# A hybrid decoder step on one core: expert rows scattered once into a sorted table, and two combinations of a pair moved around the SwiGLU transposes

## The chip, the cores and the metric

The kernel runs on one core of a Trainium2 chip. Its time is the device time of one launch in microseconds (us); lower is better. The core has TensorE (PE in the profile, PEld for its weight loads), VectorE (DVE), ScalarE (ACT), GpSimd (POOL), SyncE (SP, which here only issues transfers) and 16 DMA engines, which all queues share. All arithmetic is in float32.

## The reference, cut to what matters

One layer runs over 288 tokens: 256 of a prompt and 8 sequences of 4. After two attention-like branches and an output projection, the second half of the layer is a mixture of experts. It is the part that the change touches:

```python
def hier_moe(h, w_grp, b_grp, w_exp, b_exp, w_gate_e, w_up_e, w_down_e):
    ...                                  # top group of 4, top 2 of its 4 experts
    combine = jnp.sum(jax.nn.one_hot(expert_id, N_EXPERTS) * top_w[..., None], axis=1)
    a = jnp.einsum('td,edf->tef', t, w_gate_e)
    u = jnp.einsum('td,edf->tef', t, w_up_e)
    hid = jax.nn.silu(a) * u * combine[..., None]
    return jnp.einsum('tef,efd->td', hid, w_down_e)
```

There are 16 experts, D = 2048 and 512 hidden columns. The weights of one expert are 12.6 MB (three matrices of 2048 x 512), and the layer ends in a gated residual and an RMSNorm.

## The kernel before, in words

The kernel is written engine by engine, with semaphores; nothing reorders it. Each engine runs its own block from top to bottom, so the order of the code is the order of its queue.

Large weights come through a ring of six slots of 2 MB, loaded by SP. Over the program these are the six uses that matter here: the weights w_up_a and w_up_b ("UP", eight loads, lines 424 to 450), w_out (eight loads) and, from line 464 on, six loads per expert: gate and up of the first half of D, gate and up of the second half, and two halves of the down matrix. A load waits until PE has released the slot (`ring_free`), so the ring runs about one expert ahead of PE.

The experts are computed in *turns*. A turn takes up to 64 rows (W = 64) of one expert; an expert with more rows gets more turns, and the table `wtab` says which expert a turn has (up to 26 turns, NWIN = 26; this input needs 16). Two turns make a *pair*, and the PE loop of line 1180 runs over pairs. One turn on PE is:

1. gate and up products, 16 steps over D, two matmuls each, against the rows `hs` (lines 1186 to 1194);
2. `turn_rows`: 16 transposes of `hg`, the gathered rows of the next turn, into PSUM, from where ACT copies them to `hs`;
3. four transposes of `hid`, the SwiGLU result that DVE has made meanwhile (hid_ready), which DVE copies to `hidT`;
4. the down products, whose result ACT and DVE copy into `y_two`: one turn's 64 rows in each half of the partitions.

Rows go back to their tokens with `combine(pair, n)`, n = 0 to 7: two products of `y_two` with a matrix `spots` that has the router's weight where a row belongs to a token. DVE then adds the result to the residual `xT` (`add_pair`, line 2085), and only after that may PE start the next `combine` (`combined_read`), since all use PSUM banks 6 and 7. All eight combinations of the pair before stand between the gate and up steps of a pair's first turn.

Where the rows come from: after the router, PE turns the normalised tokens into rows, ACT copies them to `hTok`, and POOL stores them in token order in DRAM (`h_rows`, three transfers, line 625). DVE works out for each of the two choices of a token its expert's turn (`at_turn`) and its place in it (`at_slot`), PE sums them up to a list per turn (`lists_summed`), and for each turn POOL gathers 64 rows from `h_rows` by an indirect transfer (`gather`, line 627), once PE has turned the rows of the turn before. Gathered rows land in partitions 0 to 63 of `hg`.

Of the kernel before, what the change touches and what calls it, by code (L numbers as in the profile page):

```python
# [11 lines left out]
ALU = mybir.AluOpType  # L12
# [51 lines left out]
        "kv_tok_ready gla_scratch_free f_ready s_new_copied ob_ready work_free ms2_ready logits_copied member_ready pos_ready "  # L64
        "table_ready list_ready").split(),
# [7 lines left out]
def build(nc, io, out):  # L73
    with ExitStack() as ctx:
# [52 lines left out]
        h_rows = nc.dram_tensor("h_rows", [T, D], F32).ap()  # L127
# [121 lines left out]
        token_i = rstd[0:W, 0:NWIN].bitcast(I32)  # L249
        take = rstd[0:W, 64:65].bitcast(I32)  # L250
# [77 lines left out]
        def _(sp):  # L328
# [134 lines left out]
            def expert(e, turn):  # L463
# [12 lines left out]
            last_turn = sp.value_load(wtab[0:1, 1:2], min_val=NE - 1, max_val=NWIN - 3)  # L476
            with sp.Fori(0, last_turn) as w:
                e = sp.value_load(wtab[0:1, ds(w + 3, 1)], min_val=0, max_val=NE - 1)
                expert(e, w + 1)
# [11 lines left out]
        def _(pool):  # L491
# [122 lines left out]
            pool.dma_start(xflat, x_kept).then_inc(sem("x_back"), 16)  # L614
            pool.iota(iota_pos[:, :], pattern=[[1, T]], base=0, channel_multiplier=0, allow_small_or_imprecise_dtypes=True)
# [16 lines left out]
            pool.wait_ge(sem("h_stored"), 16 * NT)  # L632
            pool.wait_ge(*step("list_ready"))
            gather(0)
            pool.wait_ge(sem("hs_turned"), 1)
            gather(1)
# [3 lines left out]
            last_turn = pool.value_load(wtab[0:1, 1:2], min_val=NE - 1, max_val=NWIN - 3)  # L640
# [9 lines left out]
        def _(pe):  # L650
# [529 lines left out]
            with pe.Fori(0, pairs) as pair:  # L1180
                for half_turn in range(2):
# [22 lines left out]
                    last.then_inc(sem("hid_turned"), 1)  # L1204
                    pe.wait_ge(sem("hidT_ready"), it + 1)
# [251 lines left out]
        def _(v):  # L1457
# [582 lines left out]
            pick(at_slot, within)  # L2040
            tt(in_slot, slot_no.unsqueeze(1).to_broadcast([TT, 6, 2 * W]), at_slot.unsqueeze(2).to_broadcast([TT, 6, 2 * W]), ALU.is_equal)
            pick(at_turn, turn)
# [12 lines left out]
            v.drain()  # L2055
            for n in range(2):
                tt(listing[:, :, :, n], in_turn, entry[:, :, n:n + 1].to_broadcast([TT, 6, NWIN]), ALU.mult)
# [17 lines left out]
            copy(token_i, sums[0:W, :, 0])  # L2075
            copy(listed, sums)
            v.drain()
            v.sem_inc(reach("list_ready"), 1)

            nc.vector.memset(spots, 0.0)  # L2080
            v.wait_ge(sem("h_stored"), 16 * NT)
# [21 lines left out]
            with v.Fori(0, pairs) as pair:  # L2103
                for half_turn in range(2):
# [3 lines left out]
                    if half_turn == 0:  # L2108
                        for n in range(8):
                            add_pair(pair, n)  # L2110
# [7 lines left out]
                    copy(now[rows], listed[rows, ds(it, 1), :].rearrange("p w n -> p (w n)"))  # L2118
                    v.drain()
                    tsc(spots[rows], iota_pos[rows], now[rows, 0:1], now[rows, 1:2], ALU.is_equal, ALU.mult)  # L2120
                    v.wait_ge(sem("hid_turned"), it + 1)
                    copy(hidT, ps[:, 3, 0:4 * W].rearrange("p (f t) -> p f t", f=4)).then_inc(sem("hidT_ready"), 1)
# [42 lines left out]
```

## Time and profile before

| what | value |
| --- | --- |
| median of 3 runs | 1935.51 us (1934.56 to 1939.46) |
| span of the profiled execution | 1934.0 us (the page gives no other time of it) |
| PE busy | 1767.3 us, 91% |
| DVE, ACT, POOL busy | 28%, 11%, 8% |
| DMA moved | 531.09 MB, mean 275 GB/s |
| chain that ended last | PE 65%, issue 12%, DMA 10%, DVE 5% |
| UP and w_out stages | about 1055 to 1328 us of the span |
| router | about 1337 to 1374 us |
| loop over pairs | 1377.55 to 1904 us |
| end | to 1934.0 us |

PE is busy in nearly all of the program, but "busy" holds matmuls at either clock and with waits inside. A stage is read by what ends its waits, and by whether the DMA engines are full in it.

### The profile page before, as it was taken

The numbers are of one execution on the slowest core, as the hardware profiler recorded it, in microseconds if no ns is written. First come the engines' busy times: TensorE is split into PE (matmuls) and PEld (weight loads), VectorE is DVE, ScalarE is ACT, GpSimd is POOL, SyncE is SP. The second block draws the span as 40 slices with busy tenths as digits, with TensorE's granted clock in tenths as the row PEclk, the third lists the DMA queues.
The fourth block names the chain that finished last, engine by engine and source line by source line (L and its number), as shares of the span: only waits on it lengthen the run. The fifth ranks groups of instructions, "written<-read, shape, count | busy, mean of one in ns | idle before, by whom it ended". The sixth has DMA issues, their size and how long they took to land.

```text
span 1934.0 us, 27785 instructions
## 1 busy us (share of the span) xinstructions
PE 1767.3 (91%) x11144; PEld 1114.0 (58%) x11144; DVE 534.1 (28%) x1152; ACT 210.8 (11%) x405; POOL 156.1 (8%) x274
## 2 busy tenths in 40 slices
PE   7799999999998999978889999997699998998998
PEld 4366666666666877756667777775333333333335
DVE  3100000000047744455553111003323222231233
ACT  2010000000001201102222100002110001000002
POOL 1011111111110001410000000000100000000000
PEclk9899999999999999988899999998799899999999
DMA  9997887677516335538999874242499999999992
GB/s 371 402 380 273 317 297 285 246 262 289 198 49 201 100 111 168 207 119 298 385 392 368 325 271 134 88 174 94 146 368 406 397 397 384 410 404 383 401 391 96
DMA packets 154570, 531.09 MB, mean 275 GB/s; under 512 B 17701, under 2 KB 61899, under 8 KB 131803
## 3 DMA queue, kind: packets, MB, share of 16 engines
q1 hardware_dynamic: 128834, 432.24, 58.9%
q0 software_dynamic: 17088, 97.15, 14.1%
q10 hardware_dynamic: 8578, 0.73, 0.4%
q8 instruction: 49, 0.80, 0.2%
q14 instruction: 21, 0.17, 0.0%
HBM read 510.94 MB, written 19.15 MB: 274 GB/s over the span
## 4 chain that ended last, share of the span: by engine, by line
PE 65%; issue 12%; DMA 10%; DVE 5%; SPq 4%; DVEq 1%; POOL 1%; ACT 1%; POOLq 1%; ACTq 0%; PEldq 0%
PE ps L652 62%; DMA ring<-in_w_up_e_dram 4%; DMA ring<-in_w_ada_dram 2%; PE ps L662 2%; SPq L399 2%; DMA xT<-in_w_ada_dram 2%; SPq L393 2%; DMA xT<-in_w_in_dram 2%; POOL work L537 1%; DVE z L1468 1%; DVE z L1459 1%; DVEq L2115 1%; DVE ring L1465 1%; POOLq L536 0%; DVE ring L1837 0%
## 5 line engine op out<-in xcount | busy, mean ns | idle before, releaser
L652 PE MATMUL ps<-hT,ring 128*128 128x288 f32 x2304 | 585.3, 410 | 5.3 <-PE ps L652 3.6
L652 PEld LDWEIGHTS ps<-hT,ring 128*128 128x128 f32 x2304 | 430.0, 190 | 169.7 <-issue 59.1
L652 PE MATMUL ps<-ring,work 128*64 128x512 f32 (+1 forms) x1280 | 273.4, 617 | 25.3 <-DMA ring<-in_w_ada_dram 12.2
L652 PE MATMUL ps<-z,ring 128*128 128x288 f32 (+1 forms) x1040 | 255.5, 407 | 4.5 <-PE ps L652 2.7
L1468 DVE COPY z<-ps 128x256 f32<-128x256 f32 (+7 forms) x98 | 64.3, 660 | 677.1 <-PE ps L652 656.9
L652 PE MATMUL ps<-ring,z 32*32 32x256 f32 (+3 forms) x3744 | 213.9, 396 | 21.2 <-DVE z L1468 11.2
L652 PEld LDWEIGHTS ps<-z,ring 128*128 128x128 f32 x1040 | 196.4, 190 | 62.8 <-issue 7.5
L652 PEld LDWEIGHTS ps<-ring,work 128*64 128x64 f32 (+1 forms) x1280 | 77.8, 134 | 181.4 <-issue 165.7
L652 PEld LDWEIGHTS ps<-ring,z 32*32 32x32 f32 (+3 forms) x3744 | 108.5, 114 | 115.2 <-issue 108.3
L1263 ACT ACTIVATE z<-ps 128x512 f32<-128x512 f32 (+4 forms) x108 | 60.1, 602 | 860.3 <-PE ps L652 850.4
L1465 DVE SCALAR_TENSOR_TENSOR xT<-ps,modT,xT 128x256 f32<-128x256 f32 x160 | 70.8, 480 | 254.3 <-PE ps L652 254.2
L662 PE MATMUL ps<-ident,z 64*128 64x64 f32 (+4 forms) x644 | 91.3, 286 | 40.9 <-DVE z L1459 29.6
L662 PEld LDWEIGHTS ps<-ident,z 64*128 64x128 f32 (+4 forms) x644 | 75.7, 177 | 64.4 <-issue 48.8
L652 PE MATMUL ps<-z 128*128 128x288 f32 (+3 forms) x408 | 109.2, 393 | 2.5 <-DVEq L2126 1.5
L652 PE MATMUL ps<-hT,xT 128*128 128x288 f32 (+1 forms) x352 | 86.6, 409 | 24.7 <-DMA xT<-in_w_in_dram 24.7
L652 PEld LDWEIGHTS ps<-z 128*128 128x128 f32 (+1 forms) x408 | 64.4, 188 | 71.6 <-DVEq L2096 47.0
L652 PEld LDWEIGHTS ps<-hT,xT 128*128 128x128 f32 (+1 forms) x352 | 65.9, 203 | 43.9 <-DMA xT<-in_w_in_dram 26.4
L1263 ACT ACTIVATE work<-ps 128x512 f32<-128x512 f32 (+1 forms) x75 | 36.7, 513 | 384.7 <-PE ps L652 336.4
L1837 DVE STREAM_TRANSPOSE ring<-ring 128x2048 f32<-128x2048 f32 x32 | 72.3, 2293 | 8.0 <-issue 3.7
L628 POOL COPY rstd<-rstd 64x1 int32 (+1 forms) x17 | 3.2, 189 | 471.3 <-PE ps L662 461.8
L1459 DVE TENSOR_TENSOR hT<-hT,ps 128x288 f32<-128x288 f32 x32 | 14.5, 454 | 89.5 <-PE ps L652 88.7
L1863 DVE CUSTOM_DVE_ANT_0 xT<-ps,z 128x1024 f32<-128x1024 f32 x16 | 20.5, 1283 | 67.2 <-PE ps L652 65.9
(209 smaller groups left out, 877.4 us busy)
## 6 DMA issues: line engine op xcount, KB each, us to landing
ring<-in_w_in_dram SPq DMA_DIRECT2D x36, 2048.0 KB, 14.3
ring<-in_w_gate_e_dram SPq DMA_DIRECT2D x32, 2048.0 KB, 12.7
ring<-in_w_up_e_dram SPq DMA_DIRECT2D x32, 2048.0 KB, 18.4
ring<-in_w_down_e_dram SPq DMA_DIRECT2D x32, 2048.0 KB, 15.0
ring<-in_w_ada_dram SPq DMA_DIRECT2D x16, 2048.0 KB, 20.5
z<-in_w_ada_dram POOLq DMA_DIRECT2D x32, 1024.0 KB, 7.9
xT<-in_w_ada_dram POOLq DMA_DIRECT2D x32, 1024.0 KB, 6.7
ring<-in_cache_v_dram SPq DMA_DIRECT2D x64, 512.0 KB, 5.8
```

The lines of the kernel that those rows point to most:

```text
L393: pg = sp.value_load(ptab[0:1, ds(b * NPG + (s % 2 * 4 + n), 1)], min_val=0, max_val=io["cache_k"].shape[1] - 1)
L399: sp.dma_start(slot(s)[:, n * 1024:(n + 1) * 1024], io[name][0, ds(pg, 1)].rearrange("a p h d -> (a p) (h d)")).then_inc(sem(f"kv_full{s}" ...
L537: pool.dma_start(lf_in[:, ds(i * 2 + k // NPG, 1), k % NPG, :].rearrange("p a h -> p (a h)"), io["cache_logf"][0, ds(pg, 1)].rearrange("a ...
L652: return nc.tensor.matmul(o, lhsT, rhs, start=start, stop=stop, skip_group_check=free)
L662: return nc.tensor.transpose(o, i, ident[0:n, 0:n])
L1263: return nc.scalar.activation(o, i, func, **kw)
L1459: return nc.vector.tensor_tensor(o, a, b, op)
L1465: return nc.vector.scalar_tensor_tensor(out=o, in0=a, scalar=s, in1=b, op0=op0, op1=op1)
L1468: return nc.vector.tensor_copy(o, a)
L1837: nc.vector.transpose(kT[:, g, 4 * half:4 * half + 4], slot(half).rearrange("p (n g e) -> p n g e", n=4, g=2)[:, :, g]).then_inc(sem("keys ...
L1863: nc.vector.tensor_tensor_reduce(pS[:, g, 0:PAST].rearrange("p (a m) -> p a m", a=4), ps[:, 0:4, g * 256:(g + 1) * 256], r_turn[:, g, :].r ...
L2115: v.drain()
```

## The change

There are two parts.

First, the rows. A DRAM table `h_sorted` of 26 x 64 rows takes the place of `h_rows`. POOL fills it with zeros once (a memset of 128 x 1024, and 13 transfers of 1 MB each, right after `xT` is fetched back). When DVE has the place of each choice (`places` = turn x 64 + slot), POOL scatters the rows of `hTok` into it, six indirect transfers of 96 rows, one for each third of the tokens and each choice. SP then fetches 64 consecutive rows for a turn with a plain transfer: the first two ahead of the loop, and in the loop between the gate and up loads and the down loads of an expert. POOL's loop is gone, as are DVE's cast of the list and the signal `list_ready`. DVE picks `at_turn` before it makes `in_slot`.

Second, the order. Of the eight combinations of a pair, numbers 6 and 7 leave the gate and up steps. Number 6 now stands between `turn_rows` and the transposes of `hid`, number 7 behind these transposes. DVE's `add_pair` 6 and 7 are moved to match, and the making of `spots` goes behind them.

```diff
-            for c in range(NT):
-                pool.wait_ge(sem("htok_copied"), 4 * c + 4)
-                pool.dma_start(h_rows[c * TT:(c + 1) * TT, :], hTok[:, c, :]).then_inc(sem("h_stored"), 16)
-            def gather(w):
-
-                pool.tensor_copy(take, token_i[:, ds(w, 1)])
-                pool.drain()
-                pool.indirect_dma_start(hg, None, h_rows, bass.IndirectOffsetOnAxis(ap=take, axis=0)).then_inc(sem("hg_full"), 16)
...
+            pool.memset(cleared, 0.0)
+            pool.drain()
+            for n in range(NWIN * W // P):
+                pool.dma_start(h_sorted[n * P:(n + 1) * P, :].rearrange("p (a n) -> p a n", a=2),
+                               cleared.unsqueeze(1).to_broadcast([P, 2, 1024])).then_inc(sem("rows_cleared"), 16)
...
+            pool.wait_ge(*step("places_ready"))
+            pool.wait_ge(sem("htok_copied"), 4 * NT)
+            pool.wait_ge(sem("rows_cleared"), 16 * (NWIN * W // P))
+            for i in range(2 * NT):
+                pool.indirect_dma_start(h_sorted, bass.IndirectOffsetOnAxis(ap=places[:, i:i + 1], axis=0),
+                                        hTok[:, i // 2, :], None).then_inc(sem("rows_sorted"), 16)
...
-            with pool.Fori(0, last_turn) as it:
-                pool.wait_ge(sem("hs_turned"), it + 2)
-                gather(it + 2)
...
+            def sorted_rows(turn):
+
+                sp.dma_start(hg, h_sorted[ds(turn * W, W), :]).then_inc(sem("hg_full"), 16)
...
+                    if n == 4 and rows_of is not None:
+                        sp.wait_ge(sem("hs_turned"), rows_of)
+                        sorted_rows(rows_of)
...
             expert(0, 0)
+            sp.wait_ge(sem("rows_sorted"), 16 * 2 * NT)
+            sorted_rows(0)
+            sp.wait_ge(sem("hs_turned"), 1)
+            sorted_rows(1)
...
-                            if k % 2 and half_turn == 0:
-                                combine(pair, 4 * half + k // 2)
+                            n = 4 * half + k // 2
+                            if k % 2 and half_turn == 0 and n < 6:
+                                combine(pair, n)
...
                     turn_rows()
+                    if half_turn == 0:
+                        combine(pair, 6)
                     pe.wait_ge(sem("hid_ready"), it + 1)
...
                     last.then_inc(sem("hid_turned"), 1)
+                    if half_turn == 0:
+                        combine(pair, 7)
...
             pick(at_slot, within)
+            pick(at_turn, turn)
+            stt(places, at_turn, float(W), at_slot, ALU.mult, ALU.add)
+            v.drain()
+            v.sem_inc(reach("places_ready"), 1)
...
-            v.wait_ge(sem("h_stored"), 16 * NT)
+            v.wait_ge(sem("rows_sorted"), 16 * 2 * NT)
             nc.vector.memset(y_two, 0.0)
```

On PE the place is the end of a pair's first turn. The rows "128x64" are transposes (16 of the next rows, four of `hid`), "128x288" a combination, "ring,work" gate and up, "ring,z" down. Before:

```order
L652 MATMUL ps<-z 128x288 [waits combined_read]
L652 MATMUL ps<-z 128x288
L652 MATMUL ps<-ring,work 64x512 x4
L1170 REGISTER_ALU
L652 MATMUL ps<-z 128x288 [waits combined_read]
L652 MATMUL ps<-z 128x288
L1197 REGISTER_ALU
L662 MATMUL ps<-ident,z 128x64 [waits hg_full]
L662 MATMUL ps<-ident,z 128x64 x15
L662 MATMUL ps<-ident,z 128x64 [waits hid_ready]
L662 MATMUL ps<-ident,z 128x64 x3
L1210 REGISTER_ALU [waits y_copied_too,y_copied,hidT_ready]
```

and now:

```order
L656 MATMUL ps<-ring,work 64x512 x8
L1202 REGISTER_ALU
L666 MATMUL ps<-ident,z 128x64 [waits hg_full]
L666 MATMUL ps<-ident,z 128x64 x15
L1174 REGISTER_ALU
L656 MATMUL ps<-z 128x288 [waits combined_read]
L656 MATMUL ps<-z 128x288
L666 MATMUL ps<-ident,z 128x64 [waits hid_ready]
L666 MATMUL ps<-ident,z 128x64 x3
L1174 REGISTER_ALU
L656 MATMUL ps<-z 128x288 [waits combined_read]
L656 MATMUL ps<-z 128x288
```

Two combinations have left the gate and up steps; one now stands ahead of the wait for `hid`, one behind the transposes of `hid`.

On POOL the place is the router, from the fetching back of `xT` to the loop. "DMA h_sorted<-work" is the clearing, "DMA h_sorted<-z,rstd" the scatter. Before:

```order
L614 DMA xT<-x_kept 128x4608 [waits dve_step]
L615 IOTA z 128x288
L616 AFFINE_SELECT z<-ones 96x96
L618 IOTA work 96x6
L620 IOTA z 96x128
L625 DMA h_rows<-z 96x2048 [waits htok_copied] x3
L628 COPY rstd<-rstd 64x1 [waits dve_step,h_stored]
L630 DMA z<-h_rows,rstd 64x2048
L628 COPY rstd<-rstd 64x1 [waits hs_turned]
L630 DMA z<-h_rows,rstd 64x2048
```

and now:

```order
L625 DMA xT<-x_kept 128x4608 [waits dve_step]
L626 MEMSET work 128x1024
L629 DMA h_sorted<-work 256x1x1024 x13
L631 IOTA z 128x288
L632 AFFINE_SELECT z<-ones 96x96
L634 IOTA work 96x6
L636 IOTA z 96x128
L643 DMA h_sorted<-z,rstd 1664x2048 [waits rows_cleared,htok_copied,dve_step]
L643 DMA h_sorted<-z,rstd 1664x2048 x5
```

Thirteen transfers are added behind `xT`'s, and six scatters stand where three stores and the first gathers stood.

On SP the place is the loop over experts. Now it reads:

```order
L479 DMA ring<-in_w_gate_e_dram 128x4096
L479 DMA ring<-in_w_up_e_dram 128x4096 [waits ring_free1]
L472 REGISTER_ALU
L465 ISA [waits hs_turned]
L465 DMA z<-h_sorted 64x2048
L474 REGISTER_ALU
L479 DMA ring<-in_w_down_e_dram 128x4096 [waits ring_free2]
L479 DMA ring<-in_w_down_e_dram 128x4096 [waits ring_free3]
```

The wait for `hs_turned` and the fetch stand in SP's queue ahead of the two down loads; before, the down loads followed the up load directly.

## Rows read from the trace of the kernel before

**Rows 1.** Page, part 1: span and instructions of the profiled execution.
```profile
span 1934.0 us, 27785 instructions
```

**Rows 2.** Windows: length; PE, PEld, DVE, ACT, POOL busy; PE clock, DMA share, GB/s.
```profile
1442.80:1840.50 397.70, 363.85 (x1586) 145.63 (x1583) 111.30 (x277) 33.36 (x49) 15.45 (x24) 0.95 1.01 396
...
1840.50:1904.00 63.50, 59.76 (x264) 23.84 (x264) 17.17 (x46) 4.37 (x7) 1.45 (x2) 0.95 0.80 320
```

**Rows 3.** Waits from 1375 to 1900: engine line <- waited for: total, times, longest.
```profile
PE ps L662 <- DVE z L1459: 18.3, 16, 1.8
...
PE ps L652 <- DMA ring<-in_w_up_e_dram: 11.7, 4, 4.1
PE ps L652 <- DVE z L1468: 11.2, 16, 0.8
```

**Rows 4.** DMA queues from 1375 to 1900: packets, MB, share of 16 engines.
```profile
q1 hardware_dynamic: 12960, 188.75, 89.6%
```

**Rows 5.** DMA queues from 1448 to 1466, weights alone.
```profile
q1 hardware_dynamic: 523, 7.72, 100.7%
```

**Rows 6.** Windows of 2 us: first turn, and the end of the weights' stream.
```profile
1392.00:1394.00 2.00, 2.00 (x10) 0.49 (x8) 1.24 (x4) 0.00 (x0) 0.00 (x0) 1.00 0.85 254
1402.00:1404.00 2.00, 2.00 (x11) 0.80 (x8) 0.76 (x4) 0.50 (x1) 0.00 (x0) 1.00 0.35 147
1404.00:1406.00 2.00, 2.00 (x17) 1.61 (x15) 1.30 (x5) 0.09 (x1) 0.00 (x0) 1.00 0.80 246
...
1890.00:1892.00 2.00, 2.00 (x12) 0.61 (x10) 0.00 (x0) 0.00 (x0) 0.00 (x0) 1.00 0.41 172
```

**Rows 7.** Windows of 0.5 us while x_sample's 32 rows pass SP's queue.
```profile
8.50:9.00 0.50, 0.00 (x0) 0.00 (x0) 0.07 (x1) 0.39 (x1) 0.00 (x0) 1.00 1.00 411
9.00:9.50 0.50, 0.00 (x0) 0.00 (x0) 0.50 (x1) 0.00 (x0) 0.00 (x0) 1.00 1.38 303
9.50:10.00 0.50, 0.00 (x0) 0.00 (x0) 0.50 (x1) 0.00 (x0) 0.00 (x0) 1.00 0.81 148
10.00:10.50 0.50, 0.00 (x0) 0.00 (x0) 0.50 (x1) 0.00 (x0) 0.00 (x0) 1.00 0.90 197
10.50:11.00 0.50, 0.00 (x0) 0.00 (x0) 0.50 (x1) 0.00 (x0) 0.00 (x0) 1.00 1.00 279
```

**Rows 8.** Windows of 2 us: the first gather, alone on the DMA engines.
```profile
1370.00:1372.00 2.00, 0.00 (x0) 0.00 (x0) 0.00 (x0) 0.00 (x0) 0.00 (x0) 0.50 0.91 213
1372.00:1374.00 2.00, 0.00 (x0) 0.00 (x0) 0.00 (x0) 0.00 (x0) 0.00 (x0) 0.50 0.22 49
```

**Rows 9.** Timeline of router and loop start: start us, us, engine, line, [idle before].
```profile
1360.29 0.25 DVE L1961 TENSOR_REDUCE work<-work 96x6 f32<-96x96 f32 x1
...
1368.74 0.98 POOL L630 DMA_INDIRECT z<-h_rows,rstd  x1 [1.15 <-issue]
...
1374.15 2.03 PE L662 MATMUL ps<-ident,z 64*128 64x64 f32 x16 [7.25 <-DMA z<-h_rows,rstd]
```

**Rows 10.** DMA queues from 1351 to 1364: three stores of 96 rows each.
```profile
q0 software_dynamic: 336, 2.36, 57.4%
```

**Rows 11.** Timeline of a first turn's end.
```profile
1467.05 2.00 PE L662 MATMUL ps<-ident,z 64*128 64x64 f32 x16
...
1470.86 0.66 PE L662 MATMUL ps<-ident,z 64*128 64x64 f32 x4 [1.81 <-DVE z L1459]
...
1472.12 8.57 PE L652 MATMUL ps<-ring,z 128*64 128x512 f32 x32 [0.59 <-DVE z L1468]
```

**Rows 12.** DMA queues from 1090 to 1096: xT coming back beside UP loads.
```profile
q0 software_dynamic: 111, 1.88, 74.1%
q1 hardware_dynamic: 130, 0.55, 22.2%
```

**Rows 13.** DMA queues from 1080 to 1100.
```profile
q1 hardware_dynamic: 2006, 4.67, 64.7%
```

**Rows 14.** Timeline of PE in UP: 64 matmuls for a load, the fifth.
```profile
1132.96 15.76 PE L652 MATMUL ps<-z,ring 128*128 128x288 f32 x64 [0.30 <-PE ps L652]
```

More of the change, by code:

```diff
@@ L63 @@
         "gla_sample_ready os_turned_copied ms_a_ready rs_a_ready rs_a_inverted "
-        "kv_tok_ready gla_scratch_free f_ready s_new_copied ob_ready work_free ms2_ready logits_copied member_ready pos_ready "
-        "table_ready list_ready").split(),
+        "kv_tok_ready gla_scratch_free f_ready s_new_copied ob_ready work_free ms2_ready logits_copied member_ready places_ready pos_ready "
+        "table_ready").split(),
 }
@@ L125, in build @@
         eps_col = vcol[:, 150:151]
-        h_rows = nc.dram_tensor("h_rows", [T, D], F32).ap()
+        h_sorted = nc.dram_tensor("h_sorted", [NWIN * W, D], F32).ap()
         x_kept = nc.dram_tensor("x_kept", [P, KT * T], F32).ap()
@@ L248, in build @@
         now = ms[:, 2 * NWIN:2 * NWIN + 2]
-        token_i = rstd[0:W, 0:NWIN].bitcast(I32)
-        take = rstd[0:W, 64:65].bitcast(I32)
+        places = rstd[0:TT, 0:2 * NT].bitcast(I32)
+        cleared = work2[:, 0:1024]
         spots = z[:, 3 * D:3 * D + T]
@@ L460, in _, with expert @@
                              src.rearrange("(k p) n -> p k n", p=P)).then_inc(sem(f"ring_full{(WOUT + n) % SLOTS}"), 16)
-            def expert(e, turn):
+            def sorted_rows(turn):
+                sp.dma_start(hg, h_sorted[ds(turn * W, W), :]).then_inc(sem("hg_full"), 16)
+            def expert(e, turn, rows_of=None):
                 for n in range(6):
                     s = (MOE + n) % SLOTS
+                    if n == 4 and rows_of is not None:
+                        sp.wait_ge(sem("hs_turned"), rows_of)
+                        sorted_rows(rows_of)
                     sp.wait_ge(sem(f"ring_free{s}"), turn + freed(MOE + n))
@@ L478, in _ @@
                 e = sp.value_load(wtab[0:1, ds(w + 3, 1)], min_val=0, max_val=NE - 1)
-                expert(e, w + 1)
+                expert(e, w + 1, w + 2)
             for c in range(NT):
@@ L622, in _ @@
             pool.sem_inc(sem("route_consts_ready"), 1)
-            for c in range(NT):
-                pool.wait_ge(sem("htok_copied"), 4 * c + 4)
-                pool.dma_start(h_rows[c * TT:(c + 1) * TT, :], hTok[:, c, :]).then_inc(sem("h_stored"), 16)
-            def gather(w):
-                pool.tensor_copy(take, token_i[:, ds(w, 1)])
-                pool.drain()
-                pool.indirect_dma_start(hg, None, h_rows, bass.IndirectOffsetOnAxis(ap=take, axis=0)).then_inc(sem("hg_full"), 16)
[L632 to L636, printed above, removed]
+            pool.wait_ge(*step("places_ready"))
[4 more added lines that the diff above has]
+                                        hTok[:, i // 2, :], None).then_inc(sem("rows_sorted"), 16)
             pool.wait_ge(sem("htok_turned"), 4 * NT)
@@ L639, in _ @@
                                vcol[:, V_GF:V_GF + KT].unsqueeze(2).to_broadcast([P, KT, P]), ALU.mult).then_inc(sem("gf_spread"), 1)
-            last_turn = pool.value_load(wtab[0:1, 1:2], min_val=NE - 1, max_val=NWIN - 3)
-            with pool.Fori(0, last_turn) as it:
-                pool.wait_ge(sem("hs_turned"), it + 2)
-                gather(it + 2)
             pool.wait_ge(sem("gla_prompt_stored"), 16)
@@ L2040, in _ @@
             pick(at_slot, within)
+            pick(at_turn, turn)
+            stt(places, at_turn, float(W), at_slot, ALU.mult, ALU.add)
+            v.drain()
+            v.sem_inc(reach("places_ready"), 1)
             tt(in_slot, slot_no.unsqueeze(1).to_broadcast([TT, 6, 2 * W]), at_slot.unsqueeze(2).to_broadcast([TT, 6, 2 * W]), ALU.is_equal)
-            pick(at_turn, turn)
             tt(in_turn, iota_pos[0:TT, 0:NWIN].unsqueeze(1).to_broadcast([TT, 6, NWIN]), at_turn.unsqueeze(2).to_broadcast([TT, 6, NWIN]), ALU.is_equal)
@@ L2055, in _ @@
             v.drain()
+            v.wait_ge(sem("rows_cleared"), 16 * (NWIN * W // P))
             for n in range(2):
@@ L2074, in _ @@
             v.wait_ge(*step("lists_summed"))
-            copy(token_i, sums[0:W, :, 0])
             copy(listed, sums)
-            v.drain()
-            v.sem_inc(reach("list_ready"), 1)
             nc.vector.memset(spots, 0.0)
-            v.wait_ge(sem("h_stored"), 16 * NT)
+            v.wait_ge(sem("rows_sorted"), 16 * 2 * NT)
             nc.vector.memset(y_two, 0.0)
@@ L2108, in _ @@
                     if half_turn == 0:
-                        for n in range(8):
+                        for n in range(6):
                             add_pair(pair, n)
@@ L2118, in _ @@
                     copy(now[rows], listed[rows, ds(it, 1), :].rearrange("p w n -> p (w n)"))
+                    if half_turn == 0:
+                        add_pair(pair, 6)
+                    v.wait_ge(sem("hid_turned"), it + 1)
+                    copy(hidT, ps[:, 3, 0:4 * W].rearrange("p (f t) -> p f t", f=4)).then_inc(sem("hidT_ready"), 1)
+                    if half_turn == 0:
+                        add_pair(pair, 7)
                     v.drain()
                     tsc(spots[rows], iota_pos[rows], now[rows, 0:1], now[rows, 1:2], ALU.is_equal, ALU.mult)
-                    v.wait_ge(sem("hid_turned"), it + 1)
-                    copy(hidT, ps[:, 3, 0:4 * W].rearrange("p (f t) -> p f t", f=4)).then_inc(sem("hidT_ready"), 1)
                     v.wait_ge(*used(MOE + 4, it))
```

## Prediction

> **What bounds the kernel now.** I read the page first: a span of 1934.0 us [rows 1]. The median of the runs is 1.5 us above it; sums are made against the span, and the difference is applied to 1935.5. Then the loop, by windows. In pairs 1 to 6 the DMA engines are full: share 1.01 at 396 GB/s [rows 2]. The waits name DMA only four times, 11.7 us in all, beside 29.5 us for DVE's work on `hid` (18.3 and 11.2) [rows 3]. That looks like a PE-bound loop, but the two are tied: PE frees a slot, the load queues, and six pairs take 397.7 us, 66.3 each, while pair 7, whose loads have mostly run out (share 0.80), takes 63.5 [rows 2]. So the middle goes at the pace of the transfers, and PE has about 3 us per pair to spare.
>
> What a pair's transfers take: 15 experts load 188.75 MB [rows 4], 25.2 MB per pair. Weights alone pass at 7.72 MB in 18 us, 429 GB/s [rows 5], so 58.7 us of 66.3. The other 7.6 us are two gathers, 3.8 us each, for 0.52 MB that at 429 GB/s would take 1.2. The whole stream agrees: it runs from 1392.0 to about 1890.8, idle for some 1.7 us in the first turn [rows 6]; 497 less 188.75 / 0.429 = 440 leaves 57 for 15 gathers.
>
> **The rows: what it costs ahead of the loop.** Before, PE starts on the first rows at 1374.15 [rows 9]. Now:
> - `places`: DVE's reduction for `at_slot` ends at 1360.54 [rows 9]. A multiply and a reduction for `at_turn`, 0.25 each as that one, and a small operation, with their drains: 1361.5.
> - POOL takes some 0.8 us to the first scatter. The gather issued at 1368.74 had its bytes moving at about 1370.2 [rows 8, 9], so the scatter's move from about 1363.8.
> - The scatter moves 2 x 288 rows of 8 KB, 4.72 MB. No row shows an indirect store. The stores of the same 96-partition rows moved 2.36 MB in 57.4% of 13 us, 7.5 us, 316 GB/s [rows 10]: 14.9 us, to 1378.7. The bounds: 429 GB/s gives 11 us [rows 5]. The other end is the gather's pace: its 64 rows took some 3.1 us from 1370.2 until about 0.9 us before PE had them at 1374.15, so 576 rows need 28 us [rows 8, 9]. I take 14.9, the nearest row by partitions and direction. POOL's issue, 0.98 us for 64 rows [rows 9], is 9 us for 576 and lies beside it.
> - Receipt about 1 us, then SP's fetch: issue and first byte 1.0, 2.3 for the bytes (0.91 + 0.22 of 2 us windows, the gather alone [rows 8]), receipt 1: 1384.2.
>
> That is 10.0 us late (6 to 23), and nothing hides it: the engines and queues are idle there. DVE's memset of `y_two` now waits for the scatter too, but ends near 1382, ahead of the first combination. The queue's pauses earlier in the router stay.
>
> **The clearing.** 13.6 MB of writes follow `xT` on POOL's queue from about 1096, in pieces of 4 KB, beside UP loads in pieces of 2 KB. In [rows 12] the engines served 111 pieces of 18 KB and 130 of 2 KB, about one for one: at 1.2 small per large (2.4 KB against 4), UP loads keep 37% of 400 GB/s, 145. They have to deliver, in order, 7.5 MB by 1133.0, when PE turns to the fifth load [rows 14], and 5.4 MB by 16.1 us earlier, 1116.9. By 1100 they had moved 4.67 MB [rows 13], so at 1096 about 3.2; 2.2 MB at 145 GB/s is 15 us, 1111, and the next at 1125. Then clearing ends near 1150 with loads still 8 us early. I take 0; with UP loads at 75 GB/s, somewhat under what they had in [rows 12], the second would be 5 us late, so 6 us is the upper end. The Trainium skill (DMA: Bandwidth & Descriptors, Queues, rings and completion order) says that an engine goes round its queues by packets of several descriptors. By it the share could come out more even, and the cost would still be 0; no row here separates the two.
>
> **The fetch in the loop.** The gather on POOL's queue goes; 64 rows of 8 KB come on SP's queue, behind the gate and up loads. The bytes and the 64 partitions are the same. Its new cost is bounded below by the gather alone, 2.3 us [rows 8], and above by the 3.8 of now. The nearest row is x_sample: 32 rows of 8 KB to 32 partitions, in line on SP's queue among large loads. In the 2 us from 9.0 the mean is 232 GB/s against 411 [rows 7]: 0.87 us lost, 0.64 for its own bytes, 1.5 us. Twice is 3.0, with ragged edges counted twice. I take 2.8: 1.0 us less per turn, for 14 turns (the last is not waited for), 14.0. Nor is it late: it lands 2.8 us behind the second gate and up loads, and PE works 7 us on these. SP's new wait for `hs_turned` holds up only the down loads; their slots come free later still, since PE turns the rows before the down products.
>
> The Trainium skill (SBUF — State Buffer, Door 1: The DMA port swizzle) says that partitions 0 to 63 reach only half of the ports, about 218 GB/s, whatever queue issues. The trace agrees: 213 GB/s in the gather alone [rows 8]. By it the fetch takes 2.4 us, and moving it to SP's queue does not make it faster by itself; what can be saved is the loss of mixing.
>
> **The combinations.** Before, PE ends the row transposes at 1469.05, waits 1.81 us for `hid`, 0.59 for `hidT`, and then has 8.57 us of down products [rows 11], where turns at full clock throughout need about 7.1. The granted clock fell to its lower level (1.2 GHz) behind these waits; that is some 4 us. Combination 6 now fills the first wait, 7 the second, but 7 must wait until DVE has read 6, about 1 us. I count 3 us saved on PE per pair. The work of the combinations is the same, only moved. But PE already has slack: a pair of transfers will be 58.7 + 5.6 = 64.3 us, PE's own pair 63.5 - 3 = 60.5. So these 3 us go into waiting for DMA. What remains: in the first turn the second half's slots come free 2.6 us earlier, which removes the 1.7 us of idle queue [rows 6]. Bounds: 0 and 24 (8 x 3).
>
> **Sum.** +10.0 + 0 - 14.0 - 1.7 = -5.7 us; the span to 1928.3, the median to 1929.8.
>
> **The rivals.**
> - *Fetching costs what the gather cost* (3.8 us): the loss would be in the partitions, not in the mixing. Then the loop gains only 1.7 and perhaps 1.5 at its end. +7: 1942.5. For it: bytes and partitions are the same. Against: the gather alone and x_sample are both cheaper per row.
> - *The scatter goes at the gather's pace* and takes 28 us, not 15: +13, net +7.6, 1943. This is the slower side as one mechanism: its place is the wait of SP ahead of the first fetch, and it decides from a scatter of about 20.6 us on. For it: the only indirect transfer seen ran slower than the plain stores. Against: a gather writes to 64 partitions, the scatter reads from 96.
> - *The loop is PE's after all*, as the waits read [rows 3]: 8 x 3 = 24 saved, +10: 1921.5. Against: share 1.01 over six pairs [rows 2].
> - *Clearing starves UP*: +6, 1936.
>
> **Chances.** Forecast 0.47 (its own range 1922 to 1937), fetching as dear 0.14, slow scatter 0.15, PE's loop 0.14, starved UP 0.06, something else 0.04. A measurement tells 0.3% (5.8 us) from no change, so faster means below 1929.7, slower above 1941.3. The forecast lies on that border: about half of it and nearly all of PE's loop are faster, 0.41; slower are most of the two dear cases, 0.24; the rest 0.35. Eight in ten: 1919 to 1945.
>
> **What would show it.** The first `turn_rows` at about 1384 (later: the scatter). DMA share still 1.0 in the loop, and pairs of about 64.3 us; 66 would be the first rival, 61 the third. No more 2 us windows at 250 GB/s of 5 or 6 us length, but shorter dips. PE's waits for `hid` gone in first turns, waits for DMA longer instead. UP without a DMA wait. It would be wrong if the loop's length did not change, or the head cost over 20 us.

## The result and the profile after

The changed kernel takes 1975.0 us (median of 4 runs, 1969.5 to 1977.6) where the kernel before takes 1935.7: a ratio of 1.0195, interval 1.0174 to 1.0215. That is 45 us over the forecast of 1929.8, and outside its range.

The profiled executions are 42.1 us apart, the medians 39.4. The page's first line [rows 1], PE's first row transposes behind the router, and its last down products in the loop:

```profile
span 1976.1 us, 27750 instructions
...
1388.29 2.03 PE L666 MATMUL ps<-ident,z 64*128 64x64 f32 x16 [19.17 <-DMA z<-h_sorted]
...
1936.06 9.91 PE L656 MATMUL ps<-ring,z 128*64 128x512 f32 x32 [0.80 <-DVE z L1477]
```

The first `turn_rows` is 14.1 us late [rows 9]. The other 28 us arise in the loop, which ends near 1946 instead of 1904. Its middle by windows, after (PE, PEld, DVE, ACT, POOL busy; PE clock, DMA share, GB/s) [rows 2]:

```profile
1452.00:1850.00 398.00, 347.93 (x1498) 139.43 (x1496) 106.72 (x270) 30.68 (x45) 0.00 (x0) 0.93 0.98 374
```

The DMA engines are nearly as busy as before (0.98 against 1.01) and move 374 GB/s instead of 396. A turn moves 12.58 MB of weights and 0.52 MB of rows. At 374 GB/s these 13.1 MB last 35.05 us; at the 429 GB/s of weights alone [rows 5] they would last 30.56. With the 1.22 us of its own bytes at that pace, a fetch has a price of 5.7 us; the same reckoning gives 3.8 for the gather of before (396 GB/s). I use this formula for all runs below. It counts the 3% in which the engines now stand idle into the price; that is about 1 us of the 5.7. The expectations use 5.4, from the whole stream of the weights, with its ends. A pair takes some 70 us by it, where the prediction had 64.3.

The waits of PE from 1390 to 1946 (engine line <- waited for: total, times, longest) [rows 3]:

```profile
PE ps L656 <- DMA ring<-in_w_up_e_dram: 50.2, 15, 7.9
PE ps L656 <- DVE z L1477: 6.4, 8, 0.8
PE ps L656 <- DVEq L2106: 4.1, 8, 0.5
PE ps L666 <- DVE z L1468: 3.7, 8, 0.5
```

The waits for `hid` and `hidT` did fall as the combinations' part says, from 29.5 us to 10.1 (6.4 and 3.7), and 4.1 came for `add_pair`. What replaced them is the up load: 50.2 us in 15 waits, where it was 11.7 in 4. Around one fetch, by windows of 2 us:

```profile
1490.00:1492.00 2.00, 2.00 (x12) 0.72 (x10) 0.00 (x0) 0.00 (x0) 0.00 (x0) 1.00 0.96 410
1492.00:1494.00 2.00, 1.70 (x8) 0.29 (x4) 0.00 (x0) 0.00 (x0) 0.00 (x0) 1.00 1.05 299
1494.00:1496.00 2.00, 0.00 (x0) 0.00 (x0) 0.00 (x0) 0.00 (x0) 0.00 (x0) 1.00 1.23 213
1496.00:1498.00 2.00, 0.00 (x0) 0.00 (x0) 0.00 (x0) 0.00 (x0) 0.00 (x0) 1.00 0.81 164
1498.00:1500.00 2.00, 0.16 (x2) 0.19 (x4) 0.00 (x0) 0.00 (x0) 0.00 (x0) 0.51 1.02 328
```

The dip is neither short nor shallow: 8 us between 164 and 328 GB/s, with the engines marked busy. PE stands still for 6.14 us of it, and the granted clock falls to its lower level, 1.2 GHz, towards its end (0.51). SP's and PE's timelines name the load that is late:

```profile
1474.95 0.38 SPq L479 DMA_DIRECT2D ring<-in_w_up_e_dram  x1
1476.46 0.53 SPq L465 DMA_DIRECT2D z<-h_sorted  x1
...
1486.66 7.04 PE L656 MATMUL ps<-ring,work 128*64 128x512 f32 x32
1499.84 1.12 PE L656 MATMUL ps<-ring,work 128*64 128x512 f32 x2 [6.14 <-DMA ring<-in_w_up_e_dram]
```

The up load issued at 1474.95, ahead of the fetch, is the one PE waits for until 1499.84. The DMA view of these three issues, in the changed kernel and then at the same place of run e9 below, gives the time from each issue to its landing:

```profile
ring<-in_w_gate_e_dram SPq DMA_DIRECT2D x1, 2048.0 KB, 16.5
ring<-in_w_up_e_dram SPq DMA_DIRECT2D x1, 2048.0 KB, 24.7
z<-h_sorted SPq DMA_DIRECT2D x1, 512.0 KB, 25.8
```
```profile
ring<-in_w_gate_e_dram SPq DMA_DIRECT2D x1, 2048.0 KB, 11.7
ring<-in_w_up_e_dram SPq DMA_DIRECT2D x1, 2048.0 KB, 16.2
z<-h_sorted SPq DMA_DIRECT2D x1, 512.0 KB, 15.9
```

With the issue times, the up load lands 8.7 us behind the gate load here, and 4.9 behind it in e9. The fetch follows 2.5 us later (1.2 in e9), and the down load behind the fetch 4.6 us after that, no later than behind any load. So the fetch holds up the load in front of it in the same queue, and not the one behind it. The fetch itself is in time, 2.5 us behind the up load, near the 2.8 that the prediction had; PE never waits for it in the loop.

The clearing is in the trace as forecast. DMA queues from 1098 to 1150 (packets, MB, share):

```profile
q0 software_dynamic: 3203, 12.40, 58.2%
q1 hardware_dynamic: 4203, 9.07, 45.1%
```

SP's queue (UP loads, and four of 576 KB for `hT` among them) keeps 9.07 MB in 52 us, 174 GB/s; PE has no wait for a DMA there.

### The profile page after: what moved, and what is told of

Same layout as the page of the kernel before. It is cut to its first block, busy times and chain, and to the rows that moved or that the text cites. A ratio compares the mean times of both kernels' runs of the same rounds, so it can differ in the third digit from the quotient of the medians.

```text
span 1976.1 us, 27750 instructions
## 1 busy us (share of the span) xinstructions
PE 1775.6 (90%) x11144; PEld 1118.3 (57%) x11144; DVE 532.3 (27%) x1152; ACT 210.9 (11%) x405; POOL 148.9 (8%) x257
## 3 DMA queue, kind: packets, MB, share of 16 engines
q0 software_dynamic: 19600, 104.22, 14.1%
## 4 chain that ended last, share of the span: by engine, by line
PE 59%; DMA 20%; issue 11%; DVE 4%; SPq 3%; POOL 1%; ACT 1%; POOLq 1%; DVEq 1%; ACTq 0%; PEldq 0%
PE ps L656 56%; DMA ring<-in_w_up_e_dram 13%; DMA ring<-in_w_ada_dram 2%; PE ps L666 2%; DMA xT<-in_w_in_dram 2%; DMA xT<-in_w_ada_dram 2%; SPq L399 1%; SPq L393 1%; POOL work L548 1%; DMA h_sorted<-z,rstd 1%; DVE ring L1474 1%; DVE z L1477 0%; POOLq L547 0%; DVE ring L1846 0%; DVE ring L1586 0%
## 5 line engine op out<-in xcount | busy, mean ns | idle before, releaser
L656 PE MATMUL ps<-ring,work 128*64 128x512 f32 (+1 forms) x1280 | 285.4, 638 | 64.4 <-DMA ring<-in_w_up_e_dram 50.2
L1477 DVE COPY z<-ps 128x256 f32<-128x256 f32 (+7 forms) x98 | 64.3, 660 | 717.9 <-PE ps L656 695.8
L656 PE MATMUL ps<-ring,z 32*32 32x256 f32 (+3 forms) x3744 | 206.5, 394 | 16.3 <-DVE ring L1846 8.2
L656 PEld LDWEIGHTS ps<-ring,work 128*64 128x64 f32 (+1 forms) x1280 | 82.1, 138 | 232.4 <-issue 216.3
L656 PEld LDWEIGHTS ps<-z 128*128 128x128 f32 (+1 forms) x408 | 64.3, 188 | 64.0 <-DVEq L2106 36.7
L548 POOL DMA_DIRECT2D work<-in_cache_logf_dram x64 | 34.6, 541 | 45.3 <-issue 45.3
```

Of the source, the lines that this page charges most:

```text
L548: pool.dma_start(lf_in[:, ds(i * 2 + k // NPG, 1), k % NPG, :].rearrange("p a h -> p (a h)"), io["cache_logf"][0, ds(pg, 1)].rearrange("a ...
L656: return nc.tensor.matmul(o, lhsT, rhs, start=start, stop=stop, skip_group_check=free)
L1477: return nc.vector.tensor_copy(o, a)
```

## The experiments

All ratios are to the kernel before, run on the same chip.

**e1, the order alone.** The kernel before with the second part of the change and nothing else:

```diff
-                            if k % 2 and half_turn == 0:
-                                combine(pair, 4 * half + k // 2)
+                            n = 4 * half + k // 2
+                            if k % 2 and half_turn == 0 and n < 6:
+                                combine(pair, n)
 ...
+                    if half_turn == 0:
+                        combine(pair, 6)
 ...
+                    if half_turn == 0:
+                        combine(pair, 7)
 ...
```

> The kernel before with the second part of the change alone: combinations 6 and 7 moved, rows gathered as before. Theory A (the changed kernel's loop, 554 us against 526, is longer because a fetch on SP's queue costs the DMA engines 5.5 us a turn where POOL's gather cost 3.8): this kernel has the old gather, so 1932 to 1936, the loop 523 to 527 us, and PE's waits for DMA longer than the 11.7 us of before. Theory B (the new order of PE's work makes the loads land later and is what lengthens the loop): 1955 or more.

1928.95 us, ratio 0.9973 (0.9957 to 0.9989): 2 to 8 us faster, a little under the range of theory A and far from B's. In the same stretch as [rows 2], then PE's waits from 1390 to 1946:

```profile
1442.80:1840.50 397.70, 360.86 (x1603) 145.92 (x1604) 112.64 (x283) 32.36 (x48) 13.46 (x24) 0.97 1.01 400
```
```profile
PE ps L652 <- DMA ring<-in_w_up_e_dram: 28.3, 10, 4.6
```

The share is 1.01 at 400 GB/s, and PE's waits for the up load grew to 28.3 us (11.7 before) while those for DVE shrank. So most of what the order saves does hide under the transfers, as the forecast had it, with some 5 us more left over than I counted.

**e2, the rows alone.** The changed kernel with the old order of `combine` and `add_pair`.

> The changed kernel with the order of combinations of before: the first part of the change alone. Theory A: the whole loss is here, 1972 to 1980, a loop of 553 to 558 us. Theory B: the head's 14 us remain and the loop is back at 526, so about 1950.

1967.0 us, ratio 1.0158 (1.0126 to 1.0191); its interval overlaps that of the whole change. In the middle 380 GB/s, 5.2 us per fetch. It is 5 us under the range of theory A and 17 above B's time, so the order is not what slowed the kernel. Nor does it help here: with the dear fetch in place the whole change is 8 us above this run, with overlapping intervals. PE's waits show where the saving goes: those for the up load are 23.2 us here and 50.2 in the whole change, while those for `hid` and `hidT` are 29.3 and 10.1.

**e3, the sorted rows fetched on POOL's queue.** Table, clearing and scatter are those of the change; the plain fetch is POOL's.

```diff
-                expert(e, w + 1, w + 2)
+                expert(e, w + 1)
 ...
+            with pool.Fori(0, last_turn) as it:
+                pool.wait_ge(sem("hs_turned"), it + 2)
+                pool.dma_start(hg, h_sorted[ds(it * W + 2 * W, W), :]).then_inc(sem("hg_full"), 16)
```

> The changed kernel, but every fetch of 64 sorted rows is a plain transfer on POOL's queue, issued when hs_turned says so, not in line on SP's. Same source, same bytes, same 64 partitions. Theory A (the queue): a turn's rows cost 3.8 us of the DMA engines again, the loop is 523 to 528 us, 1945 to 1950 in all (head still 14 us late). Theory C (the sorted table as a source, rows next to each other in DRAM, is slow to read beside weights): 1970 or more.

**e4, the same on ScalarE's queue.** Only the loop's fetches move, to a second hardware queue.

> The changed kernel, but in the loop ScalarE issues the fetch on its own hardware queue behind its copy of the turned rows. Theory A1 (what costs is standing in one line with the weights): 1945 to 1952, as with POOL's queue. Theory A2 (what costs is how a hardware queue shares 64 partitions out over the engines, whichever ring it is): 1968 to 1980, as the changed kernel.

e3 takes 1944.4 us (1.0036, 1.0019 to 1.0052), e4 1943.5 (1.0034, 1.0022 to 1.0045). The middle of the loop in e3 and e4:

```profile
1452.00:1850.00 398.00, 363.35 (x1592) 145.90 (x1588) 110.55 (x277) 33.15 (x49) 6.11 (x12) 0.95 1.01 398
```
```profile
1452.00:1850.00 398.00, 361.38 (x1589) 145.66 (x1589) 111.00 (x277) 33.37 (x49) 0.00 (x0) 0.95 1.01 398
```

Both are as the theories of the queue (A and A1) had it, to a microsecond or two. 398 GB/s in both: 3.6 us per fetch, the gather's price. So neither the sorted table (against scattered rows) nor the kind of queue counts; what costs 30.6 us (1975.0 less 1944.4) is that the fetch stands in SP's line with the weights. And e3 less e1, 15.5 us, is the price of the rows' part without that.

**e5, the fetch to 128 partitions.** Why is a fetch so dear? The next runs, but for e6 and e10, keep it on SP's queue and change its shape or place. Here 128 half rows of 4 KB come; PE turns the old layout, so its rows are not the ones fetched.

```diff
-                sp.dma_start(hg, h_sorted[ds(turn * W, W), :]).then_inc(sem("hg_full"), 16)
+                sp.dma_start(z[:, D:D + 1024], h_sorted[ds(turn * W, W), :].rearrange("t (a n) -> (t a) n", a=2)).then_inc(sem("hg_full"), 16)
```

> The changed kernel, but SP's fetch in the loop writes the same 0.52 MB on the same queue at the same place to 128 partitions of 4 KB instead of 64 of 8 KB; PE turns the old layout, so the rows that it turns are not the ones fetched. Theory A (a fetch into half of the partitions takes the weights behind it in the same queue down to its own pace): the dear part is the 64 partitions, a turn's fetch should cost 1.2 to 1.6 us instead of 5.4, PE's waits for the up load fall under 10 us, and the time is about 1912 (1905 to 1925). Theory B (standing in line costs, whatever the partitions): 4 us or more per turn, about 1965 to 1975.

1908.6 us, ratio 0.9864 (0.9847 to 0.9881). 426 GB/s in the middle, 1.4 us per fetch: theory A.

**e9, the same 64 rows to partitions 32 to 95.** e5 changes the number of partitions and the size of the pieces together. This changes neither:

```diff
-                sp.dma_start(hg, h_sorted[ds(turn * W, W), :]).then_inc(sem("hg_full"), 16)
+                sp.dma_start(z[32:96, D:2 * D], h_sorted[ds(turn * W, W), :]).then_inc(sem("hg_full"), 16)
```

> The changed kernel, but SP's fetch writes its 64 rows of 8 KB to partitions 32 to 95 instead of 0 to 63; bytes, pieces, queue and place are the same, and PE turns partitions 0 to 63, so that 32 of the rows that it turns are old ones. Theory A (what is dear is writing to one half of the partitions alone): a range that lies across the middle should cost clearly less than 5.4 us per turn, 1.5 to 3, and the time 1905 to 1935. Rival (what is dear is that only 64 partitions are written, or pieces of 8 KB): 1965 to 1975 as the changed kernel.

1905.3 us, ratio 0.9839 (0.9820 to 0.9857): 70 us less than the changed kernel, for the same bytes, pieces, queue and place. The middle of the loop, and PE's waits for the up load from 1376 to 1920:

```profile
1452.00:1850.00 398.00, 383.07 (x1728) 155.45 (x1726) 122.88 (x313) 35.05 (x52) 0.00 (x0) 0.98 1.01 428
```
```profile
PE ps L656 <- DMA ring<-in_w_up_e_dram: 3.7, 5, 1.3
```

428 GB/s, 1.3 us per fetch, hardly over its own bytes. So what is dear is writing to partitions 0 to 63 alone. By the formula the 14 fetches make 62 of the 70 us; 5 more lie ahead of the loop, where the first rows come at 1383.42 instead of 1388.29, of which 4.0 is an earlier start of the scatter. The Trainium skill (SBUF — State Buffer, Door 1: The DMA port swizzle) says that partitions 0 to 63 reach only half of the ports; this run agrees, and shows that a range across the middle does not have the limit. The prediction cited that rule and drew from it only that the fetch would not get faster by itself. It did not ask what the weights in the same line would lose.

**e8, half of the rows.** The change, with 32 rows per fetch to partitions 0 to 31; the other half of a turn's rows is left out.

```diff
-                sp.dma_start(hg, h_sorted[ds(turn * W, W), :]).then_inc(sem("hg_full"), 16)
+                sp.dma_start(hg[0:32], h_sorted[ds(turn * W, 32), :]).then_inc(sem("hg_full"), 16)
```

> The changed kernel whose fetch in the loop brings 32 rows to 32 partitions instead of 64 rows to 64; half of a turn's rows are left out. Theory A (the price in line goes with the bytes into few partitions): 2.6 us per turn instead of 5.4, 1932 to 1942. Rival (a fixed price of standing in line): over 4.5 us per turn, 1960 to 1970. The row of x_sample in the trace before gave 1.5 us for 32 rows in line; if that holds, 1930 or below.

1926.5 us, ratio 0.9952 (0.9936 to 0.9969), under the 1932 to 1942 of theory A and within the "1930 or below" that I had tied to a price of 1.5. These ranges of mine were too high: e9, at 1.3 us per fetch, takes 1905.3, and e8 takes 21 us more, 1.5 per fetch, which makes 2.8 by the times. The rate is 404 GB/s in the middle; with 12.85 MB per turn that is 1.9 us lost and 0.6 of its own bytes, 2.5 us per fetch. One of them:

```profile
1514.00:1516.00 2.00, 2.00 (x10) 0.88 (x8) 0.41 (x2) 0.02 (x1) 0.00 (x0) 1.00 0.96 410
1516.00:1518.00 2.00, 2.00 (x10) 0.66 (x7) 1.05 (x4) 0.00 (x0) 0.00 (x0) 1.00 1.20 348
1518.00:1520.00 2.00, 2.00 (x10) 0.79 (x10) 1.03 (x4) 0.00 (x0) 0.00 (x0) 1.00 0.96 250
1520.00:1522.00 2.00, 2.00 (x10) 0.88 (x8) 0.32 (x2) 0.00 (x0) 0.00 (x0) 1.00 0.90 311
```

By the rate, then, the price goes with the bytes and is not a fixed loss. And it is 2.5 us where I had read 1.5 from x_sample's 32 rows [rows 7]: that row was no stand-in for a fetch in this loop.

**e7, the fetch behind the down loads.** The changed kernel, with the fetch last among an expert's transfers.

```diff
-                    if n == 4 and rows_of is not None:
-                        sp.wait_ge(sem("hs_turned"), rows_of)
-                        sorted_rows(rows_of)
 ...
+                if rows_of is not None:
+                    sp.wait_ge(sem("hs_turned"), rows_of)
+                    sorted_rows(rows_of)
```

> The changed kernel with SP's fetch behind the two down loads of an expert instead of ahead of them. Theory A (the fetch slows its neighbours in the queue wherever it stands): 1970 to 1980, with the wait moved from the up load to the down or the next gate load. Rival: the cost is that it delays the up load ahead of it just when PE is short of it; then 1945 to 1955.

1964.65 us, ratio 1.0141 (1.0112 to 1.0170): between the two ranges, nearer to A's. The rate is 382 GB/s, 5.0 us per fetch. The waits from 1395 to 1860 moved:

```profile
PE ps L666 <- DMA z<-h_sorted: 46.6, 10, 8.9
```

PE no longer waits for the up load but for the fetch itself, about as long. Where it stands decides only who is late.

**e11, two pieces of 32 rows,** one ahead of each down load.

```diff
-                sp.dma_start(hg, h_sorted[ds(turn * W, W), :]).then_inc(sem("hg_full"), 16)
+                for a in halves:
+                    sp.dma_start(hg[32 * a:32 * a + 32], h_sorted[ds(turn * W + 32 * a, 32), :]).then_inc(sem("hg_full"), 16)
 ...
-                        sorted_rows(rows_of)
+                        sorted_rows(rows_of, (0,))
+                    if n == 5 and rows_of is not None:
+                        sorted_rows(rows_of, (1,))
```

> The changed kernel with each fetch as two transfers of 32 rows, the first ahead of the first down load and the second between the two down loads. Theory A (the price goes with the bytes to those partitions): 2 x 2.5 us as with 32 rows, 1965 to 1977. Rival (the price comes from 64 rows standing close together in the queue; apart they cost what a fetch on a queue of its own costs, 3.7): 1945 to 1955.

1966.8 us, ratio 1.0161 (1.0134 to 1.0187), 382 GB/s, 5.0 us: theory A. Pieces set apart cost together about what one costs; the interval overlaps that of the whole change.

**e6, the gather to 128 partitions.** If the half of the partitions is what is dear, the kernel before pays for it too. This is e1 with a gather of 128 half rows on POOL's queue. ACT writes the columns of `hTok` so that 8 transposes of 128 x 128 take the place of 16 of 64 x 64.

```diff
-                pool.indirect_dma_start(hg, None, h_rows, bass.IndirectOffsetOnAxis(ap=take, axis=0)).then_inc(sem("hg_full"), 16)
+                pool.indirect_dma_start(hg, None, h_rows.rearrange("t (a n) -> (t a) n", a=2), bass.IndirectOffsetOnAxis(ap=take, axis=0)).then_inc(sem("hg_full"), 16)
 ...
-                for k in range(KT):
-                    last = tr(ps[:, 1 + k // 8, (k % 8) * W:(k % 8 + 1) * W], hg.rearrange("t (p k) -> t k p", k=KT)[:, k, :])
+                for k in range(KT // 2):
+                    last = tr(ps[:, 1 + k // 4, (k % 4) * P:(k % 4 + 1) * P], hg[:, k * P:(k + 1) * P])
 ...
-            copy(token_i, sums[0:W, :, 0])
+            tsc(token_i, sums[:, :, 0], 2.0, upper, ALU.mult, ALU.add)
 ...
```

> The kernel before with the order of the combinations changed, whose gather on POOL's queue takes 128 half rows of 4 KB to 128 partitions instead of 64 rows of 8 KB to 64 (columns of h_rows put in an order that makes 8 transposes of 128 x 128 enough). Theory A: a gather costs 3.7 us because it reaches only half of the partitions; with 128 it costs 1.3 to 2, the loop is bound by PE, and the time is 1900 to 1915, under both kernels. Theory B (the price is in the descriptors of an indirect transfer, or in its bytes): no gain beyond the 8 transposes, 1925 to 1930 as with the order alone.

1899.75 us, ratio 0.9818 (0.9802 to 0.9835): 36 us under the kernel before, the fastest of all. The middle of the loop, and PE's waits from 1376 to 1880:

```profile
1442.80:1840.50 397.70, 362.38 (x1606) 141.59 (x1606) 120.36 (x310) 34.06 (x51) 14.91 (x26) 0.99 1.01 428
```
```profile
PE ps L653 <- DMA ring<-in_w_up_e_dram: 17.2, 7, 2.9
PE ps L663 <- DVE z L1467: 14.2, 16, 1.4
PE ps L653 <- DVE z L1476: 6.5, 8, 0.9
```

The same cure works on another queue: 1.3 us per gather instead of 3.8 before and 3.4 in e1. Pieces and number of partitions change together here; only on SP's queue does e9 part them. The loop isn't PE's, as theory A had it: it is still that of the transfers, now at the rate of weights alone.

**e10, the same gather in the old order.**

> The kernel before with the gather of 128 half rows and 8 transposes alone, and the old order of the combinations. In the run with both, the DMA engines moved 424 to 433 GB/s throughout the loop, so the loop is still theirs. Theory A (PE's savings hide under the transfers): the order brings little here, 1899 to 1905. Rival (PE binds now, and the order saves 3 us per pair as in the prediction's third rival): 1915 to 1925.

1925.9 us, ratio 0.9949 (0.9933 to 0.9966). The rival was right, to 1 us above its range. Its middle and PE's waits from 1376 to 1900:

```profile
1442.80:1840.50 397.70, 363.15 (x1554) 139.13 (x1551) 115.04 (x289) 33.40 (x49) 13.73 (x24) 0.96 0.99 412
```
```profile
PE ps L663 <- DVE z L1462: 35.2, 16, 3.2
PE ps L653 <- DVE z L1471: 11.1, 16, 0.8
```

No wait for a load is left; PE waits 46 us for DVE (20.7 in e6), and the engines fall to 412 GB/s. The order is worth 26 us here (e10 less e6), 3.3 per pair, and 7 us in e1. The gather is worth 10 us alone and 29 on top of the order (e1 less e6). Neither resource had much to give while the other stood where it was, and I had read e6's full queue as if PE could not have been the bound without the order.

**e12, the whole change mended:** table, scatter and SP's queue as in the change, with 128 half rows and 8 transposes.

```diff
-                sp.dma_start(hg, h_sorted[ds(turn * W, W), :]).then_inc(sem("hg_full"), 16)
+                sp.dma_start(hg, h_sorted[ds(turn * W, W), :].rearrange("t (a n) -> (t a) n", a=2)).then_inc(sem("hg_full"), 16)
 ...
```

> The whole change with its fetch mended: SP fetches 128 half rows of 4 KB, the columns of the table lie so that 8 transposes of 128 x 128 turn them. The loop should be that of the run with 128 partitions on SP's queue (1.5 us per turn), 1904 to 1910; the scatter ahead of the loop still costs about 9 us against the gather of 128 half rows (1899.75), so it should be slower than that one by 5 to 10 us. If the scatter route were worth something in the loop, it would be level with it.

1912.7 us, ratio 0.9880 (0.9863 to 0.9896), 428 GB/s in the middle. It is 3 us over its range and 13 over e6, where 5 to 10 were expected. The loop is as expected, the head is not. POOL's first scatter and PE's first rows in e12:

```profile
1367.50 1.63 POOL L643 DMA_INDIRECT h_sorted<-z,rstd  x1 [259.02 <-DVEq L2054]
...
1389.89 1.97 PE L666 MATMUL ps<-ident,z 128*128 128x128 f32 x8 [16.97 <-DMA z<-h_sorted]
```

The scatter begins 3.8 us later than in the changed kernel (1363.71) and 6 later than in e5 (1361.17). ACT's twelve copies to `hTok`, from 1337 to 1376, in the changed kernel and then in e12; and in e12 one of the groups of PE's transposes that feed them:

```profile
L1272 ACT ACTIVATE z<-ps 96x512 f32<-96x512 f32 x12 | 6.1, 596 | 6.9 <-PE ps L666 6.9
```
```profile
L1272 ACT ACTIVATE z<-ps 96x512 f32<-96x512 f32 x12 | 10.8, 1059 | 7.0 <-PE ps L666 7.0
...
1359.48 0.64 PE L666 MATMUL ps<-ident,hT 128*96 128x128 f32 x4 [1.79 <-ACT z L1272]
```

One copy takes 1059 ns instead of 596 when it writes the columns in the new order; e10, with such copies too, has the same 1059. PE waits for them between its transposes, and the products from which DVE makes the places come behind these: DVE reads them at 1363.10 instead of 1359.31. That is the 3.8 us. Even mended, the scatter route loses 13 us to the gather of e6.

## Why the prediction was wrong, by its own steps

**The fetch in the loop** is the step that failed. The prediction had 2.8 us per turn instead of 3.8, a gain of 14.0 us. In place of it there are 5.7, and the difference of e3 and the changed kernel is a loss of 30.6 us. That is a miss of 44.6 of the 45. That it makes up all of the 45 is luck: the head's part (e3 less e1, 15.5 against 10.0) was 5.5 too low and the order's gain (7.2 against 1.7) 5.5 too small, and the two cancel. Four things in the step were wrong:

- *Who pays.* The step priced the fetch by its own time and asked whether it lands late. It does not; the up load ahead of it in the queue does, and PE's 50.2 us of waits are for that load.
- *The bounds.* "Bounded below by the gather alone, 2.3 us, and above by the 3.8 of now": nothing in the profile forbade more. The gather's 3.8 us were measured on a queue beside the weights, and the new fetch stands in line with them. The price on the old queue was no upper bound for the new one.
- *The nearest row.* x_sample's dip [rows 7] gave 1.5 us for 32 rows; e8 shows 2.5 for 32 rows among the experts' weights. The choice of 2.8 under 3.0, for "ragged edges counted twice", went the wrong way too, since e8 and e11 show a price that goes with the bytes.
- *The rule on the half of the ports.* It was read as a limit of the fetch (2.4 us) and not for what shares its queue. The first rival, "the loss would be in the partitions, not in the mixing", named the cause, which e9 shows, but priced it at the old 3.8.

**The head** was forecast at 10.0 and is 14.1 in the profile, in its bounds of 6 to 23. Single traces tell it only to some 3 us: e1, whose head is that of before, has its first rows at 1370.83, where before has 1374.15. POOL begins at 1363.71 where my steps give 1362.3. That is 1.4 us of late start; in e5, e7 and e8 it begins at 1361.2, 1361.3 and 1360.8, so it is not the change's. From there the chain of waits runs:

```profile
1370.54 13.05 DMA h_sorted<-z,rstd
...
1383.61 4.64 DMA z<-h_sorted
```

From the first scatter's issue to the last landing 19.9 us pass, against 17.4 in my steps, and the fetch takes 4.64 against 4.3. The term that was mis-sized is the scatter, by 2.5 us. Its pace was 311 to 340 GB/s for most of its length, as the forecast's 316, and then a tail at 209 to 33; by 2 us windows it is far from the gather's pace of the second rival. POOL's queue from 1364 to 1384:

```profile
q0 software_dynamic: 672, 4.72, 73.5%
```

By medians, e3 less e1, head and whatever else comes with the table cost 15.5 us.

**The clearing** was right: 0 in UP, with SP's queue at 174 GB/s, where 145 was reckoned for UP loads alone, and no wait of PE for a load. Its reading of [rows 12] was off: 0.55 MB in 130 pieces is 4.2 KB each and not 2. The served ratio came out near its 1.2 all the same, 4203 pieces of 2.2 KB against 3203 of 3.9 KB.

**The combinations.** The mechanism was right in each part: PE's waits for `hid` went in first turns, a saving of 3 us per pair, mostly hidden by the transfers. "What remains", 1.7 us, was too small; e1 shows 2 to 8. The 3 us are borne out by e6 against e10: 3.3 per pair, and PE's waits for DVE fall by as much, from 46.3 to 20.7 us. The third rival priced the full 24 us nearly rightly (26), but under a condition that the change itself did not bring about.

**The starting point,** a loop at the pace of transfers with PE close behind, was right, and it is why the fetch counted in full: all of its loss was on the path.

**Small slips** in the sums change nothing: the head's steps add up to 1384.0 and not 1384.2, and a scatter of 28 us makes +7.4 and not +7.6.

What stays open: why 64 rows to the lower half cost 5.0 to 5.7 us in line and 3.6 beside it. The dips show the difference only in size. A fetch of e3, from 1512:

```profile
1512.00:1514.00 2.00, 2.00 (x12) 0.74 (x10) 0.00 (x0) 0.00 (x0) 0.00 (x0) 1.00 0.97 229
1514.00:1516.00 2.00, 2.00 (x12) 0.45 (x7) 0.00 (x0) 0.00 (x0) 0.00 (x0) 1.00 0.87 233
1516.00:1518.00 2.00, 0.17 (x2) 0.00 (x0) 1.22 (x1) 1.02 (x1) 0.00 (x0) 1.00 1.04 311
1518.00:1520.00 2.00, 0.00 (x0) 0.00 (x0) 0.00 (x0) 0.00 (x0) 0.00 (x0) 1.00 0.93 393
```

Three windows at 229 to 311 GB/s stand against four at 164 to 328 in the changed kernel. Which DMA engine waits for which was not measured. Open too is why x_sample's rows were cheaper; its neighbours were smaller pieces, which no run varied.

## What to carry to other kernels

A small transfer among large ones is priced by what it does to the rate of those around it: read GB/s in windows, not its bytes. When a transfer moves to another queue, its old price is no upper bound, and one to partitions 0 to 63 is a suspect wherever it stands; laid over 128 partitions, or across the middle, it cost 1.3 to 1.4 us here instead of 3.4 to 5.7. If it must stand in line, look for the damage at the transfer ahead of it. Where two resources are tied, try both cures together before judging either: 7 and 10 us alone were 36 together.

## What the runs showed of the hardware

- The same 0.52 MB in 64 pieces of 8 KB on the same queue cost 5.7 us at partitions 0 to 63 and 1.3 at partitions 32 to 95 (e9). A shift by 32 partitions removes nearly all of the price beyond the fetch's own bytes (1.2).
- A fetch to partitions 0 to 63 in line delays the load issued ahead of it, not the one behind it: up load issued at 1474.95, fetch at 1476.46, and PE waits 6.14 us for the first, which lands 8.7 us behind the gate load; the down load lands 4.6 behind the fetch.
- An indirect gather from scattered rows, a plain fetch on POOL's queue and one on ScalarE's cost about the same, 3.4 to 3.8 us (before, e1, e3, e4).
- An indirect scatter of 576 rows from 96 partitions took 19.9 us from issue to landing, 4.72 MB, at 311 to 340 GB/s in its middle, close to the 316 of plain stores of the same rows [rows 10].
- ACT's copies of 96 x 512 took 596 ns, and 1059 ns when they wrote the same columns in a permuted order (e10, e12).
